# A fused two-block transformer kernel on one core: the diagonal scores of the heads as an all-ones product

## The reference, cut to what matters

```python
def hgrn2_chunked(q, k, v, log_f):
    b_cum = jnp.cumsum(log_f, axis=3)
    causal = jnp.tril(jnp.ones((C, C), dtype=bool))[:, :, None]
    def step(S, inp):
        q_c, k_c, v_c, b_c = inp
        ...
        diff = b_c[:, :, :, None, :] - b_c[:, :, None, :, :]
        decay = jnp.exp(jnp.where(causal, diff, -jnp.inf))
        scores = jnp.einsum('bhtk,bhsk,bhtsk->bhts', q_c, k_c, decay)
        intra = jnp.einsum('bhts,bhsv->bhtv', scores, v_c)
        ...
```

## Time and profile before

| | |
|---|---|
| median of 3 runs | 1361.17 (1360.86 to 1361.28) |
| the profiled execution, its own time | 1361.01 |
| its span in the profile | 1359.3 |
| mean granted TensorE clock | 0.999 of full speed |
| PE busy | 1345.3 |
| DVE busy | 1043.2 |
| ACT busy | 797.4 |
| POOL busy | 28.9 |

### The profile page before, as it was taken

How to read it: one execution, slowest core, us unless ns; L and a number is a source line. 1 busy time by engine, 2 the same in 40 slices (tenths; PEclk the granted TensorE clock), 3 DMA queues, 4 the chain that set the end, 5 groups by cost and what they waited for, 6 DMA issues and landing times.

```text
span 1359.3 us, 24392 instructions
## 1 busy us (share of the span) xinstructions
PE 1345.3 (99%) x8590; PEld 1208.7 (89%) x8590; DVE 1043.2 (77%) x1644; ACT 797.4 (59%) x1352; POOL 28.9 (2%) x72
## 2 busy tenths in 40 slices
PE   8999999999999999999999999999999999999998
PEld 7888888989888888888899999999999998988887
DVE  5798888777666686666778898888898877666665
ACT  4445555644344364444668898898898853544444
POOL 6000000000000010000000000000000000000000
PEclk9999999999999999999999999999999999999999
DMA  8565545655555756666574444554544286566661
GB/s 267 155 195 156 157 124 173 200 194 198 186 186 191 230 150 203 186 185 186 155 187 133 132 125 129 139 147 114 147 131 123 87 211 203 173 206 198 192 186 62
DMA packets 291215, 227.80 MB, mean 168 GB/s; under 512 B 10883, under 2 KB 270165, under 8 KB 291157
## 3 DMA queue, kind: packets, MB, share of 16 engines
q1 hardware_dynamic: 291012, 226.75, 56.2%
q10 hardware_dynamic: 144, 0.26, 0.1%
HBM read 225.90 MB, written 1.08 MB: 167 GB/s over the span
## 4 chain that ended last, share of the span: by engine, by line
PE 93%; DVE 3%; ACT 2%; issue 1%; DVEq 0%; ACTq 0%; DMA 0%
PE G L2114 11%; PE M L2114 10%; PE M L2107 7%; PE M L2108 7%; PE M L2109 7%; PE G L2121 6%; PE G L2102 5%; PE M L2121 5%; PE G L2104 5%; PE G L2103 5%; PE G L2264 2%; PE M L2867 1%; PE M L2849 1%; PE G L2107 1%; PE G L2109 1%; PE G L2108 1%
## 5 line engine op out<-in xcount | busy, mean ns | idle before, releaser
L1241 DVE TENSOR_TENSOR w_lo<-w_raw,w_hi 128x2048 fp32r<-128x2048 f32 (+2 forms) x247 | 477.7, 1942 | 122.1 <-ACT w_hi L655 114.9
L655 ACT ACTIVATE w_hi<-w_raw 128x2048 fp32r<-128x2048 f32 x197 | 375.9, 1909 | 171.4 <-PE M L2121 35.2
L2102 PE MATMUL G<-xa,w_hi 128*128 128x256 f32 x592 | 176.9, 299 | 0.0
L2104 PE MATMUL G<-xa,w_lo 128*128 128x256 f32 x592 | 167.2, 283 | 0.0
L2103 PE MATMUL G<-xa,w_hi 128*128 128x256 f32 x592 | 167.0, 282 | 0.0
L2114 PE MATMUL M<-xa,w_hi 128*128 128x512 f32 x600 | 147.9, 391 | 0.0
L2114 PE MATMUL G<-xa,w_hi 128*128 128x512 f32 x568 | 141.2, 392 | 0.0
L2114 PEld LDWEIGHTS M<-xa,w_hi 128*128 128x128 f32 x600 | 111.4, 188 | 23.0
L2114 PEld LDWEIGHTS G<-xa,w_hi 128*128 128x128 f32 x568 | 104.5, 188 | 21.0 <-issue 0.5
L2107 PE MATMUL M<-w_hi,xb 128*128 128x512 f32 x300 | 117.1, 390 | 0.1
L2108 PE MATMUL M<-w_lo,xb 128*128 128x512 f32 x300 | 116.9, 390 | 0.0
(11 more groups left out here) (467 smaller groups left out, 2537.7 us busy)
## 6 DMA issues: line engine op xcount, KB each, us to landing
w_raw<-in_w_in SPq DMA_DIRECT2D x150, 512.0 KB, 4.9
w_raw<-in_ffn_w_in SPq DMA_DIRECT2D x88, 512.0 KB, 5.0
w_raw<-in_w_ff SPq DMA_DIRECT2D x64, 512.0 KB, 4.2
w_raw<-in_ffn_w_out SPq DMA_DIRECT2D x44, 512.0 KB, 4.9
w_raw<-in_w_in SPq DMA_DIRECT2D x33, 256.0 KB, 3.2
w_raw<-in_w_out SPq DMA_DIRECT2D x16, 512.0 KB, 3.8
w_raw<-in_w_branch_gdn SPq DMA_DIRECT2D x16, 512.0 KB, 5.3
w_raw<-in_w_branch SPq DMA_DIRECT2D x12, 512.0 KB, 4.5
```

What stands on the lines that cost most here:

```text
L655: nc.scalar.activation(w_hi[:, slot, :], w_raw[:, slot, :], ACT.Copy).then_inc(hi_ready, 1)
L1241: return v.tensor_tensor(dst, src, hi.bitcast(F32), ALU.subtract)
L2102: mm(out_, w[0], x[0], start=first, stop=False)
L2104: return mm(out_, w[1], x[0], start=False, stop=last_)
```

## The change: what it does

GpSimd gets a loop of 8 passes after its last instruction: it waits for `qk_ready`, multiplies `hk` by `hq` (128 x 256) into `hrs`, copies the product rounded to fp32r into tile 14 of `xb_hi`, and subtracts to get the remainder into tile 14 of `xb_lo`; the last of the three raises the new semaphore `own_ready`. On PE `level(0)` waits for `own_ready`, and two fp32r products of `ones_r` with the two parts (128 x 256 each) take the place of the two fp32 products of 128 x 128. Every row of the result then holds the sums over channels, and DVE's product with the identity leaves the same diagonal. The semaphore `slot_passed`, which nobody waits for, goes, and SP raises `waited` in its place.

```diff
+    own_hi, own_lo = xb_hi[:, 14, :], xb_lo[:, 14, :]
+    own_kq = hrs
...
-    slot_passed = sem("slot_passed")
...
+    own_ready = sem("own_ready")
...
-            sp.sem_inc(slot_passed, 1)
+            sp.sem_inc(waited, 1)
...
+
+        with pool.Fori(1, GH + 1) as i:
+            pool.wait_ge(qk_ready, i)
+            pool.sem_inc(waited, 1)
+            nc.gpsimd.tensor_tensor(own_kq, hk, hq, ALU.mult)
+            nc.gpsimd.drain()
+            nc.gpsimd.tensor_copy(own_hi, own_kq)
+            nc.gpsimd.drain()
+            nc.gpsimd.tensor_tensor(own_lo, own_kq, own_hi.bitcast(F32), ALU.subtract).then_inc(own_ready, 1)
...
                 if l == 0:
-                    pe.wait_ge(qk_ready, i)
-                    left, right = hk, hq
+                    pe.wait_ge(own_ready, i)
+                    mm(M[:, 1, 0:T], ones_r, own_hi, start=True, stop=False)
+                    mm(M[:, 1, 0:T], ones_r, own_lo, start=False, stop=True).then_inc(lev_done, 1)
+                    return
...
-                if l > 0:
-                    out_ = M[:, 0, P:T] if l == 8 else M[:, 2 - 2 * (l % 2), 0:P]
-                    mm(out_, left[:, 0:P], right[:, P:T], start=True, stop=True).then_inc(lev_done, 1)
-                    return
-                for b in range(TT):
-                    blk = slice(P * b, P * b + P)
-                    ins = mm(M[:, 1, blk], left[:, blk], right[:, blk], start=True, stop=True)
-                ins.then_inc(lev_done, 1)
+                out_ = M[:, 0, P:T] if l == 8 else M[:, 2 - 2 * (l % 2), 0:P]
+                mm(out_, left[:, 0:P], right[:, P:T], start=True, stop=True).then_inc(lev_done, 1)
```

## The result

The changed kernel takes 1364.69 (median of 9 runs, 1364.54 to 1365.47), the kernel before 1361.17 (9 runs, 1360.81 to 1361.88): ratio 1.0026, 95% interval 1.0016 to 1.0036. It is 3.5 slower. The forecast was 1365.7, and slower.

A forecast was written before the change was run, and what follows sets the result against it. The prediction took tied PE and DVE roads to bound the kernel: DVE's hold, 8 x 0.58 = 4.6, less 0.1 of PE's saving, gives +4.5, 1365.5 on the profiled execution and 1365.7 as median; range 1359.4 to 1367.3.

The forecast's parts named there:

- Two roads of equal length: Between L2949 and the next pass's second L2849, PE and DVE roads tie; PE's saving yields 0.1 in all.
- TensorE's 0.20 a pass: At level(0), two fp32r matmuls take 0.24 instead of 0.44, saving 0.20 a pass, 1.6 in eight.
- The hold: DVE's second L1796 stands until GpSimd's multiply has read its inputs: 0.58 a pass, bounds 0 and 1.0; chance 0.47.
- All of it comes into the time, in eight passes: DVE's delay reaches both L2849 places and counts fully in every pass: 8 x 0.58 = 4.6.
- a room of 0.03 at most: At the second L2849, PE's load follows L1840's end by 0.06, leaving at most 0.03 spare in pass 2.
- through L2849 and ACT's copies behind it: In pass 8, the claimed route by which DVE's delay of 0.58 reaches the time.
- the narrower one that the forecast gave itself: Time range for a DVE hold of 0.5 to 0.75 a pass: 1365.0 to 1367.3.
- GpSimd in time: GpSimd's three instructions take about 2 within 4.5 of cover before level(0), so PE's new wait costs nothing.
- The rule of the Trainium skill: Two-input DVE and SBUF-reading GpSimd instructions exclude each other for the first one's whole length; sum as forecast.
- the 0.14 of L1500: DVE's L1500, begun while GpSimd's L631 ran, was held 0.14; as a meeting's whole cost, the sum is 1.1.
- the length of L631: GpSimd's two-input row of 2048 columns took 5.57; if it stood behind L1690, its own work is 4.46.
- only at about even odds: GpSimd's multiply gets in ahead of the second L1796: forecast chance 0.47, against 0.34 for DVE not held.

The follow-up runs named there:

- 2: Changed kernel without GpSimd's loop; level(0) keeps its two fp32r products, waits for qk_ready and multiplies whatever lies in tile 14: 1360.88, ratio 0.9998 to the kernel before.
- 1: Changed kernel with GpSimd's three instructions kept, but level(0) again the two fp32 products of the kernel before: 1364.90, ratio 1.0027 to the kernel before.
- 8: Changed kernel with GpSimd waiting for dd_ready behind both subtractions, and two DVE half chunks of w_low moved behind the copies: 1359.82, ratio 0.9990 to the kernel before.
- 7: Kernel before with only two DVE half chunks of w_low moved, behind inverse(1) and behind middle(5): 1361.04, ratio 0.9999 to the kernel before.
- 5: Changed kernel with GpSimd multiplying only the first 128 of the 256 columns: 1362.98, ratio 1.0013 to the kernel before.
- 9: Changed kernel with GpSimd's multiply replaced by a copy of hk, one input of 256 columns: 1362.43, ratio 1.0010 to the kernel before.
- 6: Changed kernel with GpSimd's multiply replaced by a memset of 256 columns, which reads nothing: 1361.05, ratio 1.0000 to the kernel before.
- 3: Changed kernel with GpSimd waiting for dd_ready of middle(2) instead of qk_ready, so its multiply begins behind both subtractions: 1361.13, ratio 1.0000 to the kernel before.

## Why the prediction was right, point by point

- **Two roads of equal length.** Shown. TensorE's part alone gives nothing (2), nothing beside GpSimd's part (1), and 1.2 where DVE has room (8 against 7).
- **TensorE's 0.20 a pass.** The term was right: 0.24 against 0.44 on the chain, 0.21 between the passes of 7 and 8.
- **The hold.** The mechanism and the order were right: the first subtraction is ahead of GpSimd's multiply, the multiply is ahead of the second, and the second stands until the multiply is nearly through. Forecast 0.58, measured 0.55. It grows with the columns read (0.27 for half of them, 5), is smaller for one input (0.20, 9), is absent with a memset (6), and leaves the subtractions when the multiply comes later (3).
- **All of it comes into the time, in eight passes.** This is the term that was mis-sized. Passes 2 to 7 lose 0.52 each, and the missing 0.03 is the little by which PE's work was longer than DVE's road: where DVE sets the pace and is not held, passes are 49.24 apart (2, 3), in the kernel before 49.26. 49.24 plus the hold gives 49.79, 49.51 and 49.44 for holds of 0.55, 0.27 and 0.20; measured were 49.78, 49.51 (5) and 49.44 (9). So the place that sets the loss is the second L2849, where I had read a room of 0.03 at most. From pass 1 to pass 2 it is 0.54: 51.05 between the two L2026 where it was 50.51. But pass 8 loses next to nothing: the load of its second L2856 comes 7.01 behind L2026, where that of L2849 came 6.93 behind L2015. Its first L2856 is late, yet ACT first does L1018 for the next product (L1007 before), whose end at 1068.32 is what the copy for `inv_w(1)` goes by. The timeline of ACT in pass 8:

```profile
1067.70 0.62 ACT L1018 ACTIVATE xa<-arena 128x512 fp32r<-128x512 f32 x1
1068.34 0.56 ACT L999 ACTIVATE arena<-M 64x128 f32<-64x128 f32 x2
1068.92 0.39 ACT L1025 ACTIVATE arena<-M 128x256 f32<-128x256 f32 x1
```

  Before, the last of these (L1014) started at 1065.41, 3.51 earlier, while L2035 is 4.07 later than L2024 was (1066.39 against 1062.32). I had named the delay of pass 8 as going "through L2849 and ACT's copies behind it", and had not asked what stood ahead of those copies. The sum as it should have been: 0.54 + 6 x 0.52 = 3.7, plus 0.08 in pass 8, less the 0.16 by which the profiled execution after came earlier to pass 1: 3.6. The spans differ by 3.6, the medians by 3.5. The 1364.69 lies in the stated range, but 0.3 under the narrower one that the forecast gave itself (1365.0 to 1367.3; a hold of 0.75 in eight passes, less 0.1, ends at 1367.1 and not at 1367.3).
- **GpSimd in time.** Right in effect, off in its terms. Multiply 0.94 (0.74 alone, where I had 0.56 to 0.70), copy 0.41, subtraction 0.74, with 0.13 and 0.14 between them, for which the prediction had an estimate of 0.1 that no row had shown: 2.36 in all where it had about 2. The last ends at 768.40 in pass 2, the forecast was before 768.5, and PE never waits for `own_ready`.
- **The rule of the Trainium skill** (SBUF — State Buffer, Who interferes with whom) was cited with the 0.14 of L1500 as the lower reading. The runs agree with the rule that a two-input DVE instruction and a GpSimd instruction that reads SBUF exclude each other. They do not agree with 0.14 as the price of any meeting: the DVE instruction stands for what is left of the GpSimd instruction that got in before it, less about 0.14.
- **What is only argued**: that the 0.14 of L1500 and the length of L631 in the kernel before are the same hold. L1500 began with 0.34 of L631 left, so by the measure above it should have been held for 0.20; and 2.1 ns a column makes an estimated 4.4 of the 2048 columns of L631, near the 4.46 that the prediction had left for it. No run tests either.

## What to carry to other kernels

A busy share of 99% on TensorE does not say that TensorE alone binds. At each place where it waits for another engine, compare the releaser's end with the moment at which TensorE would have come by itself. If they meet within a few hundredths in every pass, follow the other engine back to its last wait for TensorE: as here, work saved inside that loop can be lost, and a delay put on the other road paid almost in full. Work given to GpSimd is not off the path because GpSimd is idle: ask which two-input VectorE instructions run at the moment it starts and when it ends, and start it where they are few. Here one changed wait was worth 3.6, and the saving itself had to be made room for by moving VectorE work into VectorE's idle time.

## What the runs showed of the hardware that I had not expected

- GpSimd's multiply started 0.09 after the first subtraction and was served ahead of the second one, although DVE takes its two subtractions back to back (starts 0.34 apart). This held in all 8 passes. The forecast had counted on it, but only at about even odds.
- A copy with one input of 256 columns holds for 0.20, a multiply with two for 0.55, and a multiply of 128 columns for 0.27. The multiply's hold is 2.1 ns for each column at both sizes, with no fixed part left over; the copy's, tried at one size only, is 0.8 ns a column.
- The hold ends before the GpSimd instruction does in the trace. From the start that the held DVE instruction has or would have had to GpSimd's end are 0.69, 0.41 and 0.34 for the multiply, the half multiply and the copy, and 0.37 for the chunk in pass 1 of experiment 3. The holds are 0.55, 0.27, 0.20 and 0.24, so 0.13 to 0.14 less each time. By this measure the memset, with 0.04 left, would have held nothing even if it were able to.
- It goes both ways. The multiply took 0.94 instead of 0.74 behind the first subtraction, and the rounding copy 0.51 instead of 0.41 behind the second.
